# RMS norm statistics with tokens on the partitions, in a float32 decoder layer with experts, on one core

## What is computed

```
def rmsnorm(x, w):
    xf = x.astype(jnp.float32)
    y = xf * lax.rsqrt(jnp.mean(xf * xf, axis=-1, keepdims=True) + EPS)
    return (y * w.astype(jnp.float32)).astype(x.dtype)

xn = rmsnorm(h, norm1_w)                                # norm 0, 1024 features
...
y = rmsnorm(y.reshape(...) * silu(z), ssd_norm_w)       # norm 1, 512 features
h = h + concatenate([o_gla, y]) @ w_out
h = h + peer(rmsnorm(h, norm2_w), ...)                  # norm 2, 1024 features
y_out = rmsnorm(h, final_norm_w)                        # norm 3, 1024 features
```

## Time and profile before

| | us |
|---|---|
| median of 3 runs | 2143.62 |
| lowest, highest | 2140.54, 2146.57 |
| profiled execution, time | 2141.58 |
| profiled execution, span from first to last instruction | 2139.8 |
| TensorE busy | 2025.1 (95%) |
| VectorE busy | 1211.6 (57%) |
| ScalarE busy | 621.8 (29%) |
| GpSimd busy | 1125.8 (53%) |
| mean granted clock of TensorE | 0.967 of full speed |

### The profile page before, as it was taken

One profiled execution on the slowest core, in us unless ns is written; L12 is line 12 of the kernel. 1 busy time (PEld: TensorE's weight loads), 2 busy tenths in 40 slices (PEclk: granted clock), 3 DMA queues, 4 the chain that ended last, 5 costly groups with the idle time before them and its releaser, 6 DMA issues.

```text
span 2139.8 us, 31840 instructions
## 1 busy us (share of the span) xinstructions
PE 2025.1 (95%) x12559; PEld 1858.2 (87%) x12559; DVE 1211.6 (57%) x2223; ACT 621.8 (29%) x971; POOL 1125.8 (53%) x697
## 2 busy tenths in 40 slices
PE   5999998699999999999998898999999999999996
PEld 3578777676889999999998898999999999999995
DVE  2325364733699787788343331112577777777774
ACT  2214112310332323232322322223333333333331
POOL 0023220200437778888788888774666666666300
PEclk8999998889999999999999998999999999999998
DMA  3097102022225555666555467657999999999961
GB/s 144 2 338 259 40 30 84 1 75 84 71 92 124 123 124 123 124 124 138 123 131 101 99 122 159 131 124 226 313 320 326 325 329 323 332 322 326 332 218 46
DMA packets 231733, 365.24 MB, mean 171 GB/s; under 512 B 92081, under 2 KB 157122, under 8 KB 230978
## 3 DMA queue, kind: packets, MB, share of 16 engines
q1 hardware_dynamic: 153282, 294.43, 41.3%
q0 software_dynamic: 78336, 69.25, 16.7%
HBM read 290.21 MB, written 73.38 MB: 170 GB/s over the span
## 4 chain that ended last, share of the span: by engine, by line
PE 92%; DVE 4%; DMA 2%; ACT 1%; issue 1%; POOL 0%; SPq 0%; DVEq 0%; ACTq 0%; POOLq 0%
PE bank L795 40%; PE bank L889 29%; PE bank L536 9%; PE bank L765 3%; PE bank L570 2%; PE bank L522 1%; DMA ring<-in_u 1%; PE bank L641 1%; DVE sq L1164 1%; PE bank L612 1%; DVE xn L1167 1%; PE bank L657 1%; PE bank L831 1%; PE bank L752 1%; PE bank L722 1%; PE bank L862 1%
## 5 line engine op out<-in xcount | busy, mean ns | idle before, releaser
L795 PE MATMUL bank<-xh,usp 128*128 128x288 f32 x4320 | 762.3, 298 | 32.5 <-DVE usp L1431 17.2
L1645 POOL DMA_INDIRECT gates_scratch<-gate_val,gate_at x384 | 666.1, 1735 | 159.3 <-issue 120.3
L795 PEld LDWEIGHTS bank<-xh,usp 128*128 128x128 f32 x4320 | 643.8, 191 | 35.1 <-DVE usp L1431 17.7
L889 PE MATMUL bank<-W,vsp 128*128 128x448 f32 x3072 | 622.8, 366 | 0.0
L889 PEld LDWEIGHTS bank<-W,vsp 128*128 128x128 f32 x3072 | 577.7, 188 | 44.8
L795 PE MATMUL bank<-xl,usp 128*128 128x288 f32 x2160 | 466.4, 298 | 0.0
L795 PEld LDWEIGHTS bank<-xl,usp 128*128 128x128 f32 x2160 | 352.2, 191 | 0.0
L1431 DVE TENSOR_TENSOR usp<-ring,usp 128x1024 fp32r<-128x1024 f32 x120 | 146.1, 1221 | 307.9 <-ACT usp L1062 307.6
L1539 DVE TENSOR_TENSOR vsp<-ring,vsp 128x1024 fp32r<-128x1024 f32 x128 | 156.9, 1226 | 169.0 <-ACT vsp L1127 169.0
L1069 ACT ACTIVATE gl<-bank 128x288 f32<-128x288 f32 x256 | 91.2, 409 | 553.3 <-PE bank L795 553.2
L1668 POOL DMA_INDIRECT picked<-in_v,row_index x128 | 149.7, 1169 | 184.7 <-DVE acc L1558 162.9
(11 more groups left out here) (245 smaller groups left out, 1588.8 us busy)
## 6 DMA issues: line engine op xcount, KB each, us to landing
ring<-in_u SPq DMA_DIRECT2D x128, 512.0 KB, 3.9
ring<-in_v SPq DMA_DIRECT2D x128, 512.0 KB, 5.2
hidden_scratch<-gl SPq DMA_DIRECT2D x128, 288.0 KB, 2.2
xn<-hidden_scratch SPq DMA_DIRECT2D x128, 224.0 KB, 5.9
G<-gates_scratch SPq DMA_DIRECT2D x120, 224.0 KB, 4.8
gates_scratch<-zero SPq DMA_DIRECT2D x32, 768.0 KB, 8.9
ring<-in_wproj SPq DMA_DIRECT2D x36, 512.0 KB, 3.5
gates_scratch<-gate_val,gate_at POOLq DMA_INDIRECT x384
```

Of the source, the lines that this page charges most:

```text
L795: mm = pe.matmul(bank[b + y][:, 0:PHALF], w, src[:, k, y * PHALF:(y + 1) * PHALF], start=(k == 0 and w is hi and src is xh), stop=(k == KT ...
L889: mm = pe.matmul(bank[(k + 4) % 8][:, 0:TA], w, W[:, n % 4, z, :], start=(n == 0 and w is hi and z == 0), stop=(n == NE - 1 and w is lo))
L1645: pool.indirect_dma_start(gates_flat, bass.IndirectOffsetOnAxis(ap=gate_at[0:r, i, x:x + 1], axis=0), gate_val[0:r, i, hh, x - hh * TOPK:x ...
```

## The change

The statistics of the four norms take the form of the GLA heads' norm. `norm_sum` multiplies with a tile of squares as weights and one column of ones, five products for the five token tiles, into five columns of `bank[4]`. The last token tile has 80 tokens; `norm_cols` takes the last 128 tokens for it, so that all five are full. ScalarE takes the root of 128x5 numbers and VectorE their reciprocal. A new `norm_spread` on TensorE spreads them with five products of the broadcast column with the identity, into `bank[5]` (four token tiles) and a part of `bank[4]` (the fifth). VectorE copies the two pieces from PSUM to `sq[:, 0, :]` and scales as before. The semaphores of the group norm are merged with those of the norms (`root_ready`, `rstd_ready`, `spread`), with a turn for each of the five users.

```diff
+def norm_cols(i):
+
+    a = min(P * i, T - P)
+    return slice(a, a + P)
...
+        rstat = sb(base, "rstat", [P, 2, TILES])
...
+        norm_turn, GLA_TURN = [1, 3, 4, 5], 2
...
                 pe.wait_ge(sq_ready, norm_base[m] + k + 1)
-                for y in range(2):
-                    mm = pe.matmul(bank[4 + y][:, 0:HALF], ones, sq[:, k % 2, y * HALF:(y + 1) * HALF],
-                                   start=(k == 0), stop=(k == norm_src[m][1] - 1))
+                for i in range(TILES):
+                    mm = pe.matmul(bank[4][:, i:i + 1], sq[:, k % 2, norm_cols(i)], ones[:, 0:1],
+                                   start=(k == 0 and i == 0), stop=True, skip_group_check=True)
                 mm.then_inc(sq_used, 1)
+
+            def norm_spread(m):
+
+                pe.wait_ge(rstd_ready, norm_turn[m])
+                for i in range(TILES):
+                    out = bank[5][:, cols(i)] if i < TILES - 1 else bank[4][:, P:2 * P]
+                    mm = pe.matmul(out, rstat[:, 1, i:i + 1].broadcast_to([P, P]), ident, start=True, stop=True)
+                mm.then_inc(spread, 1)
...
             for k in range(KT):
                 norm_sum(0, k)
+            norm_spread(0)
...
             for k in range(4):
                 norm_sum(1, k)
+            norm_spread(1)
             project_out(N_FEAT + 1, 0)
...
             norm_sum(2, KT - 1)
+            norm_spread(2)
...
             for k in range(KT):
                 norm_sum(3, k)
+            norm_spread(3)
...
                 act.wait_ge(sq_used, norm_base[m] + n)
-                for y in range(2):
-                    act.activation(sq[:, 0, y * HALF:(y + 1) * HALF], bank[4 + y][:, 0:HALF], ACT.Sqrt,
-                                   scale=1.0 / (n * P), bias=cc("eps")).then_inc(root_ready, 1)
+                act.activation(rstat[:, 0, :], bank[4][:, 0:TILES], ACT.Sqrt, scale=1.0 / (n * P), bias=cc("eps")).then_inc(root_ready, 1)
...
-                for y in range(2):
-                    dve.wait_ge(root_ready, 2 * m + y + 1)
-                    rstd = sq[:, 0, y * HALF:(y + 1) * HALF]
-                    link(dve.reciprocal(rstd, rstd))
+                dve.wait_ge(root_ready, norm_turn[m])
+                dve.reciprocal(rstat[:, 1, :], rstat[:, 0, :]).then_inc(rstd_ready, 1)
+                dve.wait_ge(spread, norm_turn[m])
+                dve.tensor_copy(sq[:, 0, 0:P * (TILES - 1)], bank[5][:, :])
+                link(dve.tensor_copy(sq[:, 0, P * (TILES - 1):T], bank[4][:, 2 * P - rows(TILES - 1):2 * P]))
```

More of the change, by code:

```diff
@@ L303, in build @@
         proj_done, proj_act, proj_dve = map(sem, ["proj_done", "proj_act", "proj_dve"])
-        sq_ready, sq_used, root_ready, normed = map(sem, ["sq_ready", "sq_used", "root_ready", "normed"])
+        sq_ready, sq_used, root_ready, rstd_ready, spread, normed = map(
+            sem, ["sq_ready", "sq_used", "root_ready", "rstd_ready", "spread", "normed"])
         fl_done, fl_copied, dtl_done, dtl_copied, dt_step, dt_ready, a_exp = map(
@@ L316, in build @@
             sem, ["s_zero", "local_done", "s_updated", "inter_done", "o_copied"])
-        gsq_ready, gsum_done, gvar_ready, groot_ready, grstd_ready, gbc_done, g_normed, g_mixed = map(
-            sem, ["gsq_ready", "gsum_done", "gvar_ready", "groot_ready", "grstd_ready", "gbc_done", "g_normed", "g_mixed"])
+        gsq_ready, gsum_done, gvar_ready, g_normed, g_mixed = map(
+            sem, ["gsq_ready", "gsum_done", "gvar_ready", "g_normed", "g_mixed"])
         x_reloaded, conv_link, conv_done, xc_ready, tr_done, tr_copied = map(
@@ L669, in _ @@
             mm.then_inc(gsum_done, 1)
-            pe.wait_ge(grstd_ready, 1)
+            pe.wait_ge(rstd_ready, GLA_TURN)
             pe.wait_ge(proj_act, N_FEAT)
@@ L676, in _ @@
                                    ident[0:rows(i), 0:rows(i)], start=True, stop=True)
-            mm.then_inc(gbc_done, 1)
+            mm.then_inc(spread, 1)
             pe.wait_ge(o_copied, TILES)
@@ L1009, in _ @@
             act.wait_ge(gvar_ready, 1)
-            act.activation(gstat[:, 0, :], gstat[:, 0, :], ACT.Sqrt).then_inc(groot_ready, 1)
+            act.activation(gstat[:, 0, :], gstat[:, 0, :], ACT.Sqrt).then_inc(root_ready, 1)
             conv_out(7)
@@ L1309, in _ @@
                               ALU.add).then_inc(gvar_ready, 1)
-            dve.wait_ge(groot_ready, 1)
-            dve.reciprocal(gstat[:, 1, :], gstat[:, 0, :]).then_inc(grstd_ready, 1)
-            dve.wait_ge(gbc_done, 1)
+            dve.wait_ge(root_ready, GLA_TURN)
+            dve.reciprocal(gstat[:, 1, :], gstat[:, 0, :]).then_inc(rstd_ready, 1)
+            dve.wait_ge(spread, GLA_TURN)
             for hh in range(GH):
```

## The result

Over 14 runs of each the changed kernel takes 2152.19 us in the median (2147.42 to 2166.63), the kernel before 2141.51 (2138.31 to 2147.77). The ratio is 1.0055, with a 95% interval of 1.0039 to 1.0071: 11.8 us slower, between 8.4 and 15.2. (The 11.8 is the ratio's; the two medians differ by 10.7.) The interval lies wholly above the 0.3% that can be told from no change. The forecast was +9.9 us and 2153.5.

A forecast was written before the change was run, and what follows sets the result against it. The expert products hold 69% of the span, and the change touches some 3%. Terms +5.7 + 5.5 - 1.4 + 0.6 - 0.5 = +9.9 us on a median of 2143.62 gave 2153.5 us, range 2146 to 2158.

The forecast's parts named there:

- the load sets the step of a one-column product: In the new sums and spreads, each weight load takes 0.107 us at full clock and 0.213 at half clock.
- narrow work doesn't raise the clock: Norms 0 and 3: sums stay at clock 0.50, taking 17.06 us instead of 10.62 and 10.82.
- The rival of a raised clock: Narrow products raise the clock as wide ones do: -9.8 us in all, 2133.8 us; chance 0.08.
- it lets a raised clock fall: A run of narrow sums leaves the clock where idleness would, down some 3 us after the last wide product.
- The rival in which it holds: A raised clock holds through narrow work at norm 1 and norm 2's end: +4.9 us in all, 2148.5 us; chance 0.10.
- Norm 1: Between two output projections: -1.4 us, wide products running unbroken from the spread on; bounds -0.3 and -5.1.
- The third rival: Full clock returns later than now after norms 0, 1 and 2: +3.0 us, 2156.5 us; chance 0.12.
- Tails: Norms 0 and 3, from the sums' end to the first scaling: 3.96 us instead of 4.71, -0.75 each.
- Inner sums and the end of norm 2: Norm 2: six sums between projections +0.6 us; its end, from reciprocal to first scaling, -0.5 us.
- the -1.8 for norm 2's end with the clock up: Alternative for norm 2's end if the clock stays up: -1.8 us instead of -0.5.
- Nothing else moves: Outside the norms no change in time: table load stays under the sums, group norm keeps its instructions, experts' stages shift whole.
- the five terms: Norm 0 +5.7, norm 3 +5.5, norm 1 -1.4, norm 2's inner sums +0.6 and end -0.5: +9.9 us.

The follow-up runs named there:

- the second profile: The changed kernel measured and profiled once more with no edit: median 2149.44 us, ratio 1.0044 to the kernel before; profiled execution 2149.16 us, span 2147.3.

## Why the prediction was right

- **That the load sets the step of a one-column product**, 0.107 and 0.213 us: right. 80 instructions in 17.21 and 17.24 us are 0.215 each, and 10 in 1.01 us at full clock (an inner sum) 0.101. The Trainium skill (TensorE: Matmul & The Clock Gate, section LDWEIGHTS) has one rate for a load. Norm 3 shows twice that time at 0.50.
- **That narrow work doesn't raise the clock**: right, and it is what decided. The rival of a raised clock would have given a gain of 9.8 us. Norm 3 stood at 0.50 for 16 us of gapless narrow work. The kernel with 96 columns, which has the very same loads, is the counter-proof: 10.3 us faster than before, about the price that the rival had. The advice of the Trainium skill (TensorE: Matmul & The Clock Gate, section Why this matters for your kernels), to keep TensorE busy for the full clock, thus doesn't hold for products of one column.
- **That it lets a raised clock fall**: right. It fell in the fourth sum of norm 1, where the working had put it, but 4.0 us after the last wide product and not 3: the four sums took 4.57 us where the working has 5.34. The rival in which it holds asked for narrow steps of 0.107 through the spread, and the spread took 2.50 us.
- **Norm 1**: -1.95 for -1.4, inside its bounds; the cheaper sums make the difference, less 0.4 us that the spread took over its price. The clock was back between 463 and 464 us, 2.6 to 3.6 us after the first wide product; I had allowed 3.8 (from 451.2 to 455). The other end of this term is the place of the spread, which I had priced with 0.6 us of idleness: a misplaced one costs 5.1.
- **The third rival**, a later return of the full clock, is refuted at norm 1 by the same rows. After norm 0 the small projection takes 10.77 us against 10.57 (and 9.91 in the second profile). At norm 2 the rival came true. TensorE's wide work started at 535.7 us before, and the clock was 1.00 from 540 on. Now it starts at 543.5, and over 8 us later the clock is still 0.50 (the row below). That cost nothing, which neither the rival nor the forecast had: VectorE's scalings and the pass behind them (9.50 + 6.06 us, as before) set when the experts start.

```profile
551.00:552.00 1.00, 0.97 (x3) 0.50 0.00 0
```

- **Tails**: -0.65 each for -0.75. The copies took 0.69 + 0.16 with waits, and the spread 2.52 with its result, for 0.93 and 2.43.
- **Inner sums and the end of norm 2**: +0.60 and -0.43, for +0.6 and -0.5. The first is right in its total and not in its parts. The six sums take 1.01 us against 1.00, +0.06 where +0.4 stood, and the projections behind them 8.08 against 7.97, +0.66 where 0.2 stood for loads. That the two errors cancel is luck. And the -1.8 for norm 2's end with the clock up was a slip: its own terms give -1.5, which the 96-column kernel measured.
- **"Nothing else moves"** was right of the instructions, and too bold of the time. The terms make +9.92; the first profile shows 14.7, the second (same program) 7.5, and 3.8 of the 7.2 between them is the state space part, 74.1 or 70.3 us. In both the five terms make +9.9; what is beside them is +4.8 in the first and -2.4 in the second. A sum against one profiled execution of each kernel thus carries an error of 2 to 5 us that no term accounts for. The bound of 2 to 3 us that I gave a median was small for that, though the median came out 1.3 us from the forecast. Part of that nearness is luck: the forecast stands on a median of 3 runs, 2143.62, where 14 give 2141.51, and +9.9 on that is 2151.4.

What stays open: what decides which of its two lengths the state space part takes, and whether the change alters how often each comes. The traces show where in the part the clock is down, not what sets it. That the medians differ by 10.7 us, close to the sum of the terms, speaks against a large share of it. There is a hint in the mean clock of the runs: the profile with the long part has 0.961, the second 0.964. Of the changed kernel's 20 runs six have 0.961 (2156.3 to 2158.7 us), 13 have 0.963 to 0.965 and take 2147.4 to 2153.0, and one has 0.963 and takes 2166.6, which nothing here explains. The kernel before has two such groups, too, 0.965 to 0.966 and 0.967 to 0.968, but the one profile of it says nothing of its state space part in the longer group.

## What to carry to other kernels

Price a product by the larger of its load and its columns, at the clock that it leaves behind: 80 instructions with one column took 17.2 us where the same loads with 96 took 11.4. If such products are needed, widen the moving operand at the same loads (here 19 us between the medians, for no cost seen), or take most of them away by adding on another engine first. Where TensorE must wait for a short chain on other engines, put the handover so that the wide work behind it runs in one piece; the same five products cost 5 us more when placed one group later.

## What was not expected of the hardware

- One program's profiled executions differ by 7.2 us in span (2154.5 and 2147.3), 3.8 of it in one part where TensorE works in pieces: 74.1 us at a mean granted clock of 0.74 in one, 70.3 at 0.80 in the other. The 12 runs of the kernel with only the inner norms changed lie in two groups, with medians of 2137.70 and 2143.96.
- The granted clock is recorded as 1.00 in norm 0 (80 instructions in 17.21 us), where the steps of 0.215 us are those of 0.50 elsewhere.
- With a second wait between the last square and the root, the 1.28 us of the root's table load came at 14.43 us, after the sums, and on the chain; without it they came at 10.75 us, before them, and off the chain.
